# One table of joined rows for the PEER experts: one 8 KB gather per pick, gelu over two picks, sums two slots behind the dot products

## What is computed

```python
q = (h @ wq).reshape(B, L, PEER_HEADS, 2, PEER_QDIM // 2)
...
top_s, pos = lax.top_k(cand_s, PEER_TOPK)
expert = jnp.take_along_axis(cand_i, pos, axis=-1)
gate = jax.nn.softmax(top_s, axis=-1)
...
def eval_chunk(args):                       # 128 tokens at a time
    hx, e, g = args
    a = jnp.einsum('cd,ckd->ck', hx, u_tab[e])
    return jnp.einsum('ck,ckd->cd', g * jax.nn.gelu(a), v_tab[e])
```

## Time and profile before

| | us |
|---|---|
| median of 3 timed runs | 3482.93 |
| lowest, highest | 3481.32, 3486.77 |
| span of the profiled execution | 3478.2 |
| median less span | 4.7 |
| first gather issued | 388.3 |
| first dot, last dot (start) | 392.8, 3444.4 |

### The profile page before, as it was taken

One profiled execution on the slowest core, in us unless ns is written; L12 is line 12 of the kernel. 1 busy time (PEld: TensorE's weight loads), 2 busy tenths in 40 slices (PEclk: granted clock), 3 DMA queues, 4 the chain that ended last, 5 costly groups with the idle time before them and its releaser, 6 DMA issues.

```text
span 3478.2 us, 36816 instructions
## 1 busy us (share of the span) xinstructions
PE 3001.3 (86%) x11060; PEld 1923.4 (55%) x11060; DVE 2638.9 (76%) x6261; ACT 958.6 (28%) x2019; POOL 2085.2 (60%) x2114
## 2 busy tenths in 40 slices
PE   8999899889998799788998689889998877777775
PEld 7788766456775556446766356445775532223222
DVE  6576698889857888888768898888757998845445
ACT  3341243333312233233212233333211232211111
POOL 1010375676656766766566675666556777777774
PEclk9999999989999989999999899999999999999998
DMA  5335699999999999999999999999999999999997
GB/s 179 121 122 206 255 409 409 408 403 385 409 409 409 404 398 409 409 407 386 404 408 409 409 388 409 409 409 380 409 409 409 409 407 409 409 405 388 409 409 306
DMA packets 361796, 1299.19 MB, mean 374 GB/s; under 512 B 40257, under 2 KB 44737, under 8 KB 361473
## 3 DMA queue, kind: packets, MB, share of 16 engines
q0 software_dynamic: 298960, 1087.79, 79.1%
q1 hardware_dynamic: 62640, 209.06, 15.7%
HBM read 1282.01 MB, written 14.68 MB: 373 GB/s over the span
## 4 chain that ended last, share of the span: by engine, by line
PE 37%; DMA 30%; DVE 12%; POOL 12%; issue 7%; ACT 1%; DVEq 0%; ACTq 0%; POOLq 0%
DMA heap<-table_v,heap 27%; PE ps L977 17%; POOL heap L935 12%; PE ps L1207 11%; DVE heap L2165 4%; PE ps L1144 4%; DMA heap<-table_u,heap 3%; DVE heap L1861 1%; PE ps L1037 1%; PE ps L1128 1%; PE ps L1106 1%; PE ps L1088 1%; PE ps L1018 0%; PE ps L1094 0%; ACT heap L1485 0%
## 5 line engine op out<-in xcount | busy, mean ns | idle before, releaser
L1207 PE MATMUL ps<-heap 128*128 128x512 f32 x2816 | 1436.8, 637 | 423.7 <-DMA heap<-table_v,heap 312.2
L2165 DVE CUSTOM_DVE_ANT_0 heap<-heap,ps 128x1024 f32<-128x1024 f32 x1008 | 1216.3, 1214 | 226.8 <-DMA heap<-table_u,heap 223.5
L935 POOL DMA_INDIRECT heap<-table_v,heap x1024 | 1028.7, 1005 | 581.5 <-PE ps L1207 333.1
L935 POOL DMA_INDIRECT heap<-table_u,heap x1024 | 1021.4, 997 | 485.3 <-issue 240.9
L1207 PEld LDWEIGHTS ps<-heap 128*128 128x128 f32 x2816 | 517.5, 198 | 1130.0 <-issue 841.0
L977 PE MATMUL ps<-hT,ring 128*128 128x256 f32 x3840 | 874.1, 382 | 11.1 <-DVE hT L1980 6.0
L977 PEld LDWEIGHTS ps<-hT,ring 128*128 128x128 f32 x3840 | 734.5, 192 | 174.5 <-issue 75.0
L1861 DVE SCALAR_TENSOR_TENSOR heap<-heap 128x1024 f32<-128x1024 f32 x313 | 401.6, 1283 | 273.4 <-issue 188.5
L1485 ACT ACTIVATE heap<-ident,heap 128x128 f32<-128x128 f32 x704 | 266.7, 395 | 536.1 <-PE ps L1207 320.1
L1505 ACT ACTIVATE heap<-heap 128x8 f32<-128x8 f32 x128 | 26.7, 209 | 555.5 <-DVE heap L2165 555.3
L1144 PE MATMUL ps<-temp,ring 128*128 128x256 f32 x640 | 150.5, 384 | 1.5 <-ACT temp L1359 1.0
(11 more groups left out here) (270 smaller groups left out, 2583.4 us busy)
## 6 DMA issues: line engine op xcount, KB each, us to landing
ring<-weights SPq DMA_DIRECT2D x344, 512.0 KB, 7.3
ring<-ssm_par SPq DMA_DIRECT2D x36, 512.0 KB, 8.9
heap<-table_u,heap POOLq DMA_INDIRECT x1024, 12.7
heap<-table_v,heap POOLq DMA_INDIRECT x1024, 12.6
ssm_par<-heap POOLq DMA_DIRECT2D x20, 512.0 KB, 4.9
ring<-weights SPq DMA_DIRECT2D x20, 256.0 KB, 6.3
ssm_par<-heap POOLq DMA_DIRECT2D x8, 256.0 KB, 3.0
xT<-x_cm SPq DMA_DIRECT2D x2, 512.0 KB, 4.7
```

What stands on the lines that cost most here:

```text
L935: pool.indirect_dma_start(rows[:, j, :], None, table, bass.IndirectOffsetOnAxis(expert[:, tile % 2, k:k + 1], 0)).then_inc(landed, 16)
L1207: mm = pe.matmul(ps[:, SUM_BANK + half, :], diag[:, PE_TURN[v] % DIAGS, :], rows_v[:, v % NV, half * 512:(half + 1) * 512], start=(k == 0) ...
L2165: dve.tensor_tensor_reduce(row, row, token, 1.0, 0.0, ALU.mult, ALU.add, act_st[:, g % 3, pick % GROUP:pick % GROUP + 1]).then_inc(dotted, 1)
```

## The change

- The host joins the tables: row i of `table_uv` is row i of `u` followed by row i of `v`, 8 KB. A pick needs one gather of 128 x 8 KB = 1 MB, 1024 gathers instead of 2048, with the same bytes in all.
- Eight buffers of 8 KB per partition (`NR`) replace the twelve of 4 KB. A buffer is given back when the `v` half has been summed, so a pick holds its place from the issue of its gather to the end of its sum.
- `GROUP` goes from 8 to 2, with four sets of the small arrays (`WIDE`) instead of three: 512 gelus and 512 weighs instead of 128 each. `weigh` now stands at the head of the slot that follows the second dot; before it came two slots later, behind the slot's sum and dot. The sum is placed in the second or third slot behind the group's last dot (`LAG` = 4).
- On ACT the diagonal for the next slot's sum is written at the end of a slot, behind the slot's items and its gelu; before it came first.
- "htok" for both tiles moves to the end of a stage's query work (before, that of tile 0 stood behind the first head). Even tiles' tokens go straight into the PSUM banks, only odd tiles' go to `h_tok` (now one array) and then through "hload". In stages 1 to 3 all of "htok" waits until the last dot of the stage before.
- The memory that POOL's descriptors take is cut from 16 KB to 4 KB per partition, which makes room for the larger buffers.

In the new plan the first dot stands in slot 233 and the last in slot 1269, 1284 slots in all; 698 picks are summed on PE and 326 on DVE.

```diff
-NU = 6
-NV = 6
-GROUP = 8
+NR = 8
+GROUP = 2
+WIDE = 4
-LAG = 12
+LAG = 4
+SCRATCH = 4096
...
     for h in range(PH):
         out += [("wq", u, h), ("score", u, h), ("top", 2 * u, h), ("settle", 2 * u, h)]
-        out += [("htok", u, 0, 0), ("htok", u, 0, 1)] if h == 0 else []
...
-    return out + [("htok", u, 1, 0), ("htok", u, 1, 1)]
+    return out + [("htok", u, t, half) for t in range(2) for half in range(2)]
...
-                and s - end_of[v // GROUP * GROUP + GROUP - 1] >= LAG - GROUP + 1 + v % GROUP:
+                and s - end_of[v // GROUP * GROUP + GROUP - 1] >= 2 + v % GROUP:
...
-            if item[0] == "htok" and item[2] == 1 and item[1] and u < 2 * item[1] * PICKS:
+            if item[0] == "htok" and item[1] and u < 2 * item[1] * PICKS:
...
-            for table, pick in GATHERS:
-                j = pick % NU if table == "u" else pick % NV
-                if table == "u":
-                    if pick % TOPK == 0:
-                        pool.wait_ge(picks_ready, pick // TOPK + 1)
-                    if pick >= NU:
-                        pool.wait_ge(dotted, pick - NU + 1)
-                    gather(table_u, rows_u, j, pick, u_landed[j])
-                else:
-                    if pick >= NV:
-                        pool.wait_ge(v_free[j], pick // NV)
-                    gather(table_v, rows_v, j, pick, v_landed[j])
+            for pick in range(TILES * PICKS):
+                tile, k, j = pick // PICKS, pick % PICKS, pick % NR
+                if pick % TOPK == 0:
+                    pool.wait_ge(picks_ready, pick // TOPK + 1)
+                if pick >= NR:
+                    pool.wait_ge(row_free[j], pick // NR)
+                pool.indirect_dma_start(rows[:, j, :], None, table_uv,
+                                        bass.IndirectOffsetOnAxis(expert[:, tile % 2, k:k + 1], 0)).then_inc(row_landed[j], 16)
...
             for slot, after in zip(PLAN, PLAN[1:] + [{"v": None}]):
                 g = slot["u"]
-                if after["v"] in PE_TURN:
-                    diag_of(after["v"])
...
-                    act.activation(gelu_st[:, n % 3, :], act_st[:, n % 3, :], ACT.Gelu_apprx_tanh).then_inc(gelued, 1)
+                    act.activation(gelu_st[:, n % WIDE, :], act_st[:, n % WIDE, :], ACT.Gelu_apprx_tanh).then_inc(gelued, 1)
+                if after["v"] in PE_TURN:
+                    diag_of(after["v"])
...
             for n_slot, slot in enumerate(PLAN):
+                if pending and pending[0][1] <= n_slot:
+                    weigh(pending.popleft()[0])
                 if slot["v"] in DVE_TURN:
                     sum_pick(slot["v"])
                 if slot["u"] is not None:
                     dot(slot["u"])
                     if slot["u"] % GROUP == GROUP - 1:
-                        pending.append((slot["u"] // GROUP, n_slot + 2))
-                if pending and pending[0][1] <= n_slot:
-                    weigh(pending.popleft()[0])
+                        pending.append((slot["u"] // GROUP, n_slot + 1))
```

More of the change, by code:

```diff
@@ L472, in make_plan @@
         chosen = (("settle", u // PICKS, u % PICKS // TOPK), 1 if u % GROUP == GROUP - 1 else 0)
-        there = (("hload", u // PICKS), 0) if u % PICKS >= FIRST_DOTS else (("htok", u // PICKS // 2, u // PICKS % 2, 1), 1)
+        there = (("hload", u // PICKS), 0) if u // PICKS % 2 and u % PICKS >= FIRST_DOTS else (("htok", u // PICKS // 2, u // PICKS % 2, 1), 1)
         if u < TILES * PICKS and ready([chosen, there], s) and u - v <= LAG:
@@ L547 @@
 PLAN = make_plan()
[L550 to L561, removed]
 ON_DVE = [slot["v"] for slot in PLAN if slot["v"] is not None and slot["v_on"] == "DVE"]
@@ L568, with trunk @@
 DVE_OF_TILE = [[v for v in ON_DVE if v // PICKS == tile] for tile in range(TILES)]
-def trunk(nc, x_cm, positions, inv_freq, weights, keys, vecs, log_dt, ssm_bc, pool_edge, table_u, table_v, final_g, out_cm):
+def trunk(nc, x_cm, positions, inv_freq, weights, keys, vecs, log_dt, ssm_bc, pool_edge, table_uv, final_g, out_cm):
     par = nc.dram_tensor("ssm_par", (DEPTH * len(PARS) * P, BLK), F32)
@@ L768, in trunk @@
         picks_ready = sem("picks_ready")
-        u_landed = [sem(f"u_landed{j}") for j in range(NU)]
-        v_landed = [sem(f"v_landed{j}") for j in range(NV)]
-        v_free = [sem(f"v_free{j}") for j in range(NV)]
+        row_landed = [sem(f"row_landed{j}") for j in range(NR)]
+        row_free = [sem(f"row_free{j}") for j in range(NR)]
         dotted = sem("dotted")
@@ L1207, in sum_pick @@
                     mm = pe.matmul(ps[:, SUM_BANK + half, :], diag[:, PE_TURN[v] % DIAGS, :],
-                                   rows_v[:, v % NV, half * 512:(half + 1) * 512], start=(k == 0), stop=(k == PICKS - 1))
-                mm.then_inc(v_free[v % NV], 1)
+                                   rows[:, v % NR, D + half * 512:D + (half + 1) * 512], start=(k == 0), stop=(k == PICKS - 1))
+                mm.then_inc(row_free[v % NR], 1)
             live = {}
@@ L1413, in emit @@
                     b = done_unit(item)
[L1414 to L1421, removed]
+                    if t == 0:
+                        if u:
+                            act.wait_ge(dotted, 2 * u * PICKS)
+                        else:
+                            act.wait_ge(bank_free[TOKEN_BANK + half], BANK_TOTAL[TOKEN_BANK + half])
+                        act.copy(ps[:, TOKEN_BANK + half, :], ps[:, b, :]).then_inc(h_there, 1)
+                        act.wait_ge(h_there, 4 * u + half + 1)
+                    else:
+                        if u:
+                            act.wait_ge(h_there, 4 * u)
+                        else:
+                            act.wait_ge(prep_over, 1)
+                        act.copy(h_tok[:, 512 * half:512 * half + 512], ps[:, b, :]).then_inc(h_copied, 1)
+                        act.wait_ge(h_copied, 2 * u + half + 1)
                     act.sem_inc(bank_free[b], 1)
@@ L1425, in emit @@
                     tile = item[1]
[L1426 to L1431, removed]
+                    act.wait_ge(h_copied, tile + 1)
+                    act.wait_ge(dotted, PICKS * tile)
                     for half in range(2):
-                        act.copy(ps[:, TOKEN_BANK + half, :], h_tok[:, tile % 2, 512 * half:512 * half + 512]).then_inc(h_there, 1)
+                        act.copy(ps[:, TOKEN_BANK + half, :], h_tok[:, 512 * half:512 * half + 512]).then_inc(h_there, 1)
                         yield
@@ L2154, in dot @@
             def dot(pick):
[L2155 to L2164 removed]
+                tile, k, g = pick // PICKS, pick % PICKS, pick // GROUP
+                early = tile % 2 == 1 and k < FIRST_DOTS
+                if early and k == 0:
+                    dve.wait_ge(h_copied, tile + 1)
+                elif k == (FIRST_DOTS if tile % 2 else 0):
+                    dve.wait_ge(h_there, 2 * (tile + 1))
+                if pick % GROUP == 0 and g >= WIDE:
+                    dve.wait_ge(gelued, g - WIDE + 1)
+                dve.wait_ge(row_landed[pick % NR], 16 * (pick // NR + 1))
+                row = rows[:, pick % NR, 0:D]
+                token = h_tok if early else ps[:, TOKEN_BANK:TOKEN_BANK + 2, :].rearrange("p i c -> p (i c)")
                 dve.tensor_tensor_reduce(row, row, token, 1.0, 0.0, ALU.mult, ALU.add,
[L2166 removed]
+                                         act_st[:, g % WIDE, pick % GROUP:pick % GROUP + 1]).then_inc(dotted, 1)
             def weigh(g):
@@ L2175, in weigh @@
                 dve.wait_ge(gelued, g + 1)
-                dve.scalar_tensor_tensor(w_st[:, g % 3, :], gelu_st[:, g % 3, :], share, gates[:, tile % 2, k:k + GROUP], ALU.mult,
+                dve.scalar_tensor_tensor(w_st[:, g % WIDE, :], gelu_st[:, g % WIDE, :], share, gates[:, tile % 2, k:k + GROUP], ALU.mult,
                                          ALU.mult).then_inc(weighed, 1)
```

54 lines of the change are left out of this document (19 added, 35 removed).

## The result

The changed kernel takes 3543.1 us (median; 3539.5 to 3548.0) against 3482.1 us before: ratio 1.0176, 95% interval 1.0163 to 1.0188. It is slower by 61 us, and lies 18 us above the range. The profiled execution has a span of 3544.5 us, 66.3 more than the one before.

What follows compares the result with a forecast made beforehand. The prediction took DMA bytes, a full queue at 409 GB/s, to bound the kernel. Span 3478 - 80 (rate) + 24 (start) + 27 (shorter chain) = 3449 us, so 3454 us against 3483; range 3410 to 3525.

Steps and rivals of the forecast that it cites:

- The bound and the rate: DMA queue, full at 409 GB/s, sets the time; gathers of 8 KB rows move at 422 GB/s: -80 us.
- Rival A: Gathers: 8 KB rows may move as two 4 KB pieces, no better rate; 3507 us, or 3487 with 1.1%; chance 0.15.
- term 3: Queue after the change: the shorter chain slows DVE's dense stretches, 340 slots keep the old pace: +27 us.
- The start: Before the first dot, about 444 us: gathers wait for the first sum, 10 MB are missing: +24 us.
- part 3: Whether the queue stays full: buffers held from issue to sum counted as nothing, the shorter chain as +27 us.
- part 4: Tile and stage changes: "htok" after a stage's last dot is hidden by the queue, 0, at most 9 us.
- B: DVE, ACT and PE: the chain in lockstep becomes the bound, 0.1 us per slot over 1038 slots; 3531 us; chance 0.18.
- C: DMA queue: stays full throughout, so the +27 us for the shorter chain vanish; 3427 us; chance 0.22.

Runs made afterwards that it cites:

- the run: Changed kernel with the token turn of tile 0 back behind the first head in stage 0 only: 3509.4 us, 34 us less than the changed kernel.
- the short ring: Changed kernel with four weight pieces in the ring instead of six: 3814.2 us with eight row buffers, 3781.9 us with nine.
- the short chain alone: Kernel before, with its two tables and twelve buffers, given the changed kernel's GROUP, WIDE, LAG, weigh and diagonal places, sums two slots behind: 3510.7 us against 3480.0.
- the thin run: Changed kernel gathering 512 B a row instead of 8 KB: 3280.3 us; the kernel before with 512 B rows of either table: 3310.2 us.
- no drains: Changed kernel without the drains of the first seven tiles, the next tile's sums following without a pause: 3462.6 us, 80 us less.
- the diagonal first: Changed kernel with ACT's diagonal for the next sum written at the head of the slot again: 3506.8 us, 36 us less.

## Why the prediction was wrong

**The bound and the rate** held. The queue was full at 409, 8 KB rows go at 421 to 422, and the 4.5 us of the `out_cm` store had pointed there. That the number itself was met was in part luck: only 36% of the packets' time in that window was the store's 8 KB rows, and the same reading carried through gave 447. The Trainium skill's page "DMA: Bandwidth & Descriptors" gives about 3 cycles of overhead per packet in "Why small descriptors are slow (HBM only)"; an estimate from that is 414 GB/s, and the measured 421 is higher. The same page, in "SWDGE vs HWDGE vs iDMA", has "≤4096 B preferably" for a packet; here 8 KB rows were moved whole, since POOL's queue went from 298,960 packets to 151,504 with the same bytes. Rival A is out. (The 3482 us of span that the prediction gives for the 3 cycles count term 3 at 10 us, as rival A does; with its own +27 the sum is 3499.)

**The start** held: first dot at 447 (I said 444), the window 388 to 454 at 239 GB/s, 15.8 MB where I had 15.6, and 31 us (by the windows) or 34 us (by the run) where I had 24.

**The step that failed is the one on the queue**, at two sentences. In part 3, on buffers held from issue to sum: "I count nothing for it". In part 4, on tile changes: "The dips to 385 at tile changes stay as they are". I had worked out the right quantity, about 4 rows in flight against 5, and then argued that landing time shrinks with it. It does, to 9.8 us at one gather per 3.0 us: 3.4 MB in flight. But 5.3 us is the shortest landing in that trace, so what is left as reserve is 4.5 us. Before, a median of 12.7 us with a shortest of 4.4 left 8.3 us. The sums pause 4 to 7 us at a tile change in either kernel; that fits into the second reserve and not into the first, roughly at least, since the kernel before loses 26 us there too. And before only half of the gathers waited for sums. Two runs show that the number of buffers matters this much: one less +146 us, one more -32 (beside the short ring). The tile changes alone lose 44 us more than before by the windows.

Term 3's other half, the chain, was about the right size and had the wrong contents. I counted DVE's dense stretches (+27); the short chain alone measured +31 in the kernel before. But a dense DVE by itself costs nothing: from 2924 to 3100 us, behind the trunk's last product, it is 90 to 92% busy and the rate stays at 421. The move of the diagonal behind the gelu, worth 36 us in the changed kernel, had no term of its own.

A rough sum from the single runs, an estimate since they need not add: 3482 + 31 (short chain) + 34 (start) - 57 (rate) = 3490 us. The 53 us that are left to 3543 I take for the held rows, which I had priced at nothing.

**The rivals.** B forecast the right sign from the wrong mechanism. It needed 1 us per pair on DVE; the trace shows 0.34, and the thin run is 263 us faster than the changed kernel. A part of it was real all the same: 31 us for the short chain alone, 63 us in the six tiles of the thin runs. Its price, 3531 us, was near the result by accident. C was wrong for the same reason as the forecast.

What stays open: how the 115 us split exactly. The single runs (-80, -36) may overlap, and no drains and the diagonal first were not run together. No run with more than eight buffers and the full ring fitted into the memory, and the kernel before was not run without its drains. Nor was it tested alone what it costs that in stages 1 to 3 "htok" waits for the last dot. The tiles that end a stage took 1268 us instead of 1229 (three together), the three between them 1152 instead of 1158.

## What to carry to other kernels

When a change ties a buffer's release to a later step, ask not only whether the average number in flight is enough but how long the releasing step ever pauses, and compare that with the landing time less its minimum. Look at the same place in the trace of before, too: a pause that looks like the cause may have been there already, at a lower price. A run with the transfers thinned out shows whether the engines or the queue's supply are short, but read it stretch by stretch, since another limit (here POOL's issues) can take over in one of them. And each move in an engine's order needs its own term, even one that only puts a 0.4 us instruction behind another.

## What was not expected of the hardware

- 8 KB rows by an indirect gather reach 421 to 422 GB/s in long stretches, 4 KB rows 409, with the same bytes and buffers.
- Shortening the ring of 512 KB weight pieces from six to four costs 271 us under this load, though a piece lands in a median of 8.5 us in one and 7.9 us in the other.
- At the last tile change of the changed kernel TensorE's granted clock was 0.99 from 3195 to 3200 us, and 0.50 (its level of 1.2 GHz; the other is 2.4) from 3200 to 3210, after waits of 1.3, 2.3 and 3.2 us. Sixteen matmuls (four sums) took 10.1 us where eight had taken 3.7 before it. In the kernel before it was 0.66 over 5 us and 8.8 us for sixteen.
- POOL's issue of an indirect gather took a median of 0.94 us for rows of 512 B, 4 KB and 8 KB alike, and 1.25 us from start to start when it waited for nothing.
